# Attention over selected keys: exponentials turned unscaled, the softmax factor applied to a pair's output, one output bank

## The reference, cut to what matters

```python
def dsa_attention(h, w_in, q_gain, k_gain, w_uv, w_out, rel_bias):
    ...
    def block(args):
        ...
        _, sel = lax.top_k(isc, topk)
        valid = sel <= t[None, :, None]
        kg = k[bidx, sel]
        vg = vals[bidx, sel]
        logits = jnp.einsum('bqhd,bqkd->bqhk', qb, kg) * scale
        bias = rel_bias[t5_bucket(t[None, :, None] - sel)]
        logits = logits + jnp.swapaxes(bias, -1, -2).astype(jnp.float32)
        logits = jnp.where(valid[:, :, None, :], logits, NEG_2)
        p = jax.nn.softmax(logits, axis=-1)
        return jnp.einsum('bqhk,bqkd->bqhd', p, vg)

    ...
    o = jnp.einsum('bshl,hlv->bshv', o_lat, w_uv.astype(jnp.float32))
    return o.reshape(B, S, DSA_HEADS * DSA_V_DIM).astype(h.dtype) @ w_out
```

## Time and profile before

| | |
|---|---|
| median of three runs | 1922.81 us (1921.42 to 1926.16) |
| profiled execution, own time | 1924.47 us |
| its span, first to last instruction | 1922.7 us |
| PE busy | 1891.4 us, 98% of the span |
| DVE, ACT, POOL busy | 1071.2, 530.6, 1178.2 us |
| mean granted clock of TensorE | 0.995 of full speed |
| attention stage, first score to first product of the output projection | 1421.9 to 1512.5 us |

### The profile page before, as it was taken

One profiled execution on the slowest core, in us unless ns is written; L12 is line 12 of the kernel. 1 busy time (PEld: TensorE's weight loads), 2 busy tenths in 40 slices (PEclk: granted clock), 3 DMA queues, 4 the chain that ended last, 5 costly groups with the idle time before them and its releaser, 6 DMA issues.

```text
span 1922.7 us, 27358 instructions
## 1 busy us (share of the span) xinstructions
PE 1891.4 (98%) x9550; PEld 1539.9 (80%) x9550; DVE 1071.2 (56%) x1750; ACT 530.6 (28%) x1120; POOL 1178.2 (61%) x680
## 2 busy tenths in 40 slices
PE   9999999999999999999999999999989999999999
PEld 7867788888888877779888888876866798888887
DVE  5966589877785515555534342145988454343422
ACT  4135310000115424442211121033367331111110
POOL 7641688887665564335766666655764447666673
PEclk9999899999999999999999999999999999999999
DMA  7530277776552232124332333312210123332231
GB/s 278 196 103 12 68 272 252 249 240 218 197 175 68 86 110 62 48 62 158 110 98 91 95 98 99 98 64 80 86 58 2 34 66 120 98 98 92 94 98 66
DMA packets 62328, 221.06 MB, mean 115 GB/s; under 512 B 6907, under 2 KB 7163, under 8 KB 62124
## 3 DMA queue, kind: packets, MB, share of 16 engines
q1 hardware_dynamic: 45216, 161.58, 26.7%
q10 hardware_dynamic: 17036, 58.46, 8.4%
HBM read 217.87 MB, written 2.14 MB: 114 GB/s over the span
## 4 chain that ended last, share of the span: by engine, by line
PE 93%; DVE 3%; POOL 2%; issue 2%; ACT 1%; DMA 0%; SPq 0%; POOLq 0%; DVEq 0%; ACTq 0%
PE bank L321 25%; PE bank L323 25%; PE bank L322 25%; PE bank L921 2%; PE bank L580 1%; PE bank L356 1%; PE bank L361 1%; PE bank L1050 1%; PE bank L357 1%; PE bank L1102 1%; PE bank L1093 1%; PE bank L943 1%; PE bank L426 1%; PE bank L427 1%; PE bank L430 1%
## 5 line engine op out<-in xcount | busy, mean ns | idle before, releaser
L1558 POOL TENSOR_TENSOR w_lo<-raw,w_hi 128x1024 fp32r<-128x1024 f32 (+1 forms) x304 | 762.5, 2509 | 24.8
L321 PE MATMUL bank<-a_hi,w_hi 128*128 128x512 f32 (+1 forms) x2016 | 767.8, 381 | 0.8 <-POOL w_lo L1558 0.5
L322 PE MATMUL bank<-a_lo,w_hi 128*128 128x512 f32 (+1 forms) x2016 | 765.4, 380 | 0.0
L323 PE MATMUL bank<-a_hi,w_lo 128*128 128x512 f32 (+1 forms) x2016 | 765.4, 380 | 0.0
L1553 POOL TENSOR_SCALAR w_hi<-raw 128x1024 fp32r<-128x1024 f32 x298 | 341.4, 1146 | 608.7 <-PE bank L323 459.8
L321 PEld LDWEIGHTS bank<-a_hi,w_hi 128*128 128x128 f32 x2016 | 379.8, 188 | 72.5 <-POOL w_lo L1558 0.9
L323 PEld LDWEIGHTS bank<-a_hi,w_lo 128*128 128x128 f32 x2016 | 379.7, 188 | 71.3
L322 PEld LDWEIGHTS bank<-a_lo,w_hi 128*128 128x128 f32 x2016 | 379.9, 188 | 70.5
L2122 DVE SCALAR_TENSOR_TENSOR tmp<-bank,vecs,tmp 128x511 f32<-128x511 f32 x88 | 65.9, 749 | 240.9 <-ACT tmp L1828 240.8
L2107 DVE CUSTOM_DVE_ANT_0 y<-y,cond 128x1024 f32<-128x1024 f32 x84 | 197.7, 2388 | 0.0
L1828 ACT ACTIVATE tmp<-bank,vecs 128x512 f32<-128x512 f32 x88 | 68.1, 779 | 351.1 <-PE bank L323 347.2
(11 more groups left out here) (306 smaller groups left out, 2117.1 us busy)
## 6 DMA issues: line engine op xcount, KB each, us to landing
raw<-in_stream SPq DMA_DIRECT2D x299, 512.0 KB, 3.6
y<-in_ada ACTq DMA_DIRECT2D x96, 512.0 KB, 4.5
x<-in_x SPq DMA_DIRECT2D x4, 512.0 KB, 6.7
bias<-in_bias ACTq DMA_DIRECT2D x1, 2048.0 KB, 13.8
y<-rel_rows ACTq DMA_DIRECT2D x1, 2048.0 KB, 8.0
bias<-rel_rows ACTq DMA_DIRECT2D x1, 2048.0 KB, 14.4
out<-x SPq DMA_DIRECT2D x8, 256.0 KB, 2.0
cond<-in_c ACTq DMA_DIRECT2D x1, 512.0 KB, 6.5
```

The costliest lines, as they stand in the source:

```text
L321: pe.matmul(o, lhs_hi, rhs_hi, start=start, stop=False, **kw)
L322: pe.matmul(o, lhs_hi, rhs_lo, start=False, stop=False, **kw)
L323: return pe.matmul(o, lhs_lo, rhs_hi, start=False, stop=stop, **kw)
L1558: m = pool.tensor_tensor(w_lo[:, s, part], raw[:, j, part], f32(w_hi[:, s, part]), ALU.subtract)
```

## The change

The rows of scores are no longer scaled. ACT writes the exponentials straight into `tmp`, which frees the score bank; PE transposes them, and the outputs are sums of unscaled weights. For each pair DVE makes eight reciprocals in one instruction, widens them to a 128 by 512 tile (`factor_columns`), PE transposes that tile in four squares into bank 7, ACT copies it to `factor_rows`, and DVE multiplies the pair's output bank by it in place (`scaled`) before ACT and DVE round it as before. Bank 7 now holds the factor, so all pairs share output bank 6, and the wait for the low part of pair k stands ahead of pair k + 1. An output run now covers two blocks (four units) at a distance of six steps: two runs for a pair instead of four. Of the eight transposed units of a pair DVE copies three (units 1, 3 and 5) and ACT five; they have a place for every unit of a pair. The ring of tables has three buffers, since `first_rows` holds transposed units now. The new distances are in the diff. The new counters and the declaration of `factor_columns` are left out there, and so are the calls.

```diff
@@ -899,21 +900,43 @@
                         evacuate(u // 8 - 1)
...
         def score_bank(u):
...
-        D_NORM, D_TURN, D_COPY, D_OUT, D_HIGH, D_LOW = 2, 4, 3, 5, 9, 11
-        def pe_attention(pe, sems, units, queries, keys, values, probs, evacuated, ready=()):
+        def turned_bank(u):
+            return bank[(3, 5)[u % 2]]
+        factor_bank, d_out = bank[7], bank[6]
+        factor_rows = squares[:, 0, :]
+        def copied_by_dve(u):
+            return u % 8 in (1, 3, 5)
+        def d_probs(u):
+            i, side = u % 8 // 2, u % 2
+            return (probs_t[:, 2 + side, 384:512], first_rows[:, 256 * side:256 * side + 256], probs_t[:, 2 + side, 0:384], probs_t[:, side, :])[i]
+        def pair_ends(u):
+            return u >= 0 and u % 8 == 7
+        D_RECIPROCAL, D_TURN, D_COPY, D_COPY_DVE, D_SPREAD, D_FACTOR, D_OUT, D_SCALE, D_HIGH, D_LOW = 2, 4, 4, 4, 4, 4, 6, 7, 8, 9
+        def pe_attention(pe, sems, units, queries, keys, values, probs, base, evacuated, ready=()):
             n = len(units)
+            def copied(u):
+                mine = copied_by_dve(u)
+                pe.wait_ge(sems["copied_dve" if mine else "copied_act"], sum(copied_by_dve(k) == mine for k in range(u + 1)))
             for step in range(n + D_OUT):
...
-                        pe.wait_ge(sems["normed"], step - 3)
+                        pe.wait_ge(sems["exp"], step - 3)
                     if step == 3:
                         for counter, value in ready:
@@ -922,34 +945,44 @@
                 if D_TURN <= step < n + D_TURN:
                     u = step - D_TURN
                     h, i = units[u]
-                    pe.wait_ge(sems["normed"], u + 1)
+                    pe.wait_ge(sems["exp"], u + 1)
                     if u >= 2:
-                        pe.wait_ge(sems["copied"], u - 1)
+                        copied(u - 2)
                     for j in range(i + 1):
-                        m = pe.transpose(bank[(3, 5)[u % 2]][:, j * P:(j + 1) * P], tmp[:, u % 4, j * P:(j + 1) * P], ident)
+                        m = pe.transpose(turned_bank(u)[:, j * P:(j + 1) * P], tmp[:, u % 4, j * P:(j + 1) * P], ident)
                     m.then_inc(sems["turned"], 1)
+                u = step - D_SPREAD
+                if pair_ends(u):
+                    pe.wait_ge(sems["widened"], u // 8 + 1)
+                    if u > 7:
+                        pe.wait_ge(sems["factor"], u // 8)
+                    for i in range(TT):
+                        m = pe.transpose(factor_bank[:, i * P:(i + 1) * P], factor_columns[:, i * P:(i + 1) * P], ident)
+                    m.then_inc(sems["spread"], 1)
                 u = step - D_OUT
-                if u >= 0 and u % 2:
...
+                if u >= 0 and u % 4 == 3:
+                    h = units[u][0]
+                    copied(u - 1)
+                    copied(u)
+                    if h >= 2 and u % 8 == 3:
+                        pe.wait_ge(*evacuated(h // 2 - 1))
+                    for first in (u - 3, u - 1):
+                        i = units[first][1]
+                        for j in range(i + 1):
+                            for side in range(2):
+                                o = d_out[64 * side:64 * side + 64, i * P:(i + 1) * P]
+                                m = pe.matmul(o, values(h - 1 + side, j), probs(first + side)[:, j * P:(j + 1) * P], start=j == 0, stop=j == i)
+                                if j == i:
+                                    m.then_inc(sems["out"], 1)
+        def dve_attention(v, sems, units, tables, base, probs, low, prepared):
             n = len(units)
             for step in range(n + D_LOW):
-                u = step - D_LOW
-                if u >= 0 and units[u][0] % 2 and units[u][1] == TT - 1:
-                    low(v, units[u][0] // 2)
                 if step < n:
                     h, i = units[step]
                     cols = P * (i + 1)
@@ -962,40 +995,64 @@
                     b = score_bank(step)[:, 0:cols]
                     v.tensor_tensor_reduce(b, b, table, -1.0, 3e38, ALU.add, ALU.min,
                                            neg_max[:, base + step:base + step + 1]).then_inc(sems["masked"], 1)
-                u = step - D_NORM
...
+                u = step - D_COPY_DVE
+                if 0 <= u < n and copied_by_dve(u):
+                    cols = P * (units[u][1] + 1)
+                    v.wait_ge(sems["turned"], u + 1)
+                    if u >= 8:
+                        v.wait_ge(sems["out"], u - 7)
+                    v.tensor_copy(probs(u)[:, 0:cols], turned_bank(u)[:, 0:cols]).then_inc(sems["copied_dve"], 1)
+                u = step - D_RECIPROCAL
+                if pair_ends(u) and u < n:
                     v.wait_ge(sems["exp"], u + 1)
-                    v.reciprocal(rden[:, base + u:base + u + 1], den[:, base + u:base + u + 1]).then_inc(sems["rden"], 1)
...
+                    pair = slice(base + u - 7, base + u + 1)
+                    v.reciprocal(rden[:, pair], den[:, pair]).then_inc(sems["rden"], 1)
+                    v.wait_ge(sems["rden"], u // 8 + 1)
+                    if u > 7:
+                        v.wait_ge(sems["spread"], u // 8)
+                    v.tensor_scalar(factor_columns[:].rearrange("p (n s) -> p n s", n=8), rden[:, pair].unsqueeze(2).broadcast_to([P, 8, 64]),
+                                    1.0, None, ALU.mult).then_inc(sems["widened"], 1)
+                u = step - D_SCALE
+                if pair_ends(u) and u < n:
+                    v.wait_ge(sems["out"], u + 1)
+                    v.wait_ge(sems["factor"], u // 8 + 1)
+                    v.tensor_tensor(d_out[:], d_out[:], factor_rows, ALU.mult).then_inc(sems["scaled"], 1)
+                u = step - D_LOW
+                if pair_ends(u):
+                    low(v, u // 8)
...
         def act_attention(a, sems, units, probs, base, evacuate):
...
                     cols = P * (units[step][1] + 1)
-                    b = score_bank(step)[:, 0:cols]
                     a.wait_ge(sems["masked"], step + 1)
-                    a.activation(b, b, ACT.Exp, bias=neg_max[:, base + step:base + step + 1],
+                    if step >= 4:
+                        a.wait_ge(sems["turned"], step - 3)
+                    a.activation(tmp[:, step % 4, 0:cols], score_bank(step)[:, 0:cols], ACT.Exp, bias=neg_max[:, base + step:base + step + 1],
                                  scale=-1.0, accum_out=den[:, base + step:base + step + 1]).then_inc(sems["exp"], 1)
+                u = step - D_HIGH
+                if pair_ends(u):
+                    a.wait_ge(sems["scaled"], u // 8 + 1)
+                    evacuate(a, u // 8)
                 u = step - D_COPY
-                if 0 <= u < n:
+                if 0 <= u < n and not copied_by_dve(u):
                     cols = P * (units[u][1] + 1)
                     a.wait_ge(sems["turned"], u + 1)
-                    if u >= 4:
...
+                    if u >= 8:
+                        a.wait_ge(sems["out"], u - 7)
+                    a.activation(probs(u)[:, 0:cols], turned_bank(u)[:, 0:cols], ACT.Copy).then_inc(sems["copied_act"], 1)
+                u = step - D_FACTOR
+                if pair_ends(u) and u < n:
+                    a.wait_ge(sems["spread"], u // 8 + 1)
+                    if u > 7:
+                        a.wait_ge(sems["scaled"], u // 8)
+                    a.activation(factor_rows, factor_bank[:], ACT.Copy).then_inc(sems["factor"], 1)
@@ -1611,9 +1668,9 @@
             pool.wait_ge(selected, TT)
             for n, (h, i) in enumerate(masked_units):
                 cols = P * (i + 1)
-                if n >= 4:
-                    pool.wait_ge(d_sems["masked"], d_units.index(masked_units[n - 4]) + 1)
+                if n >= 3:
+                    pool.wait_ge(d_sems["masked"], d_units.index(masked_units[n - 3]) + 1)
                 pool.tensor_tensor(table_buf(n)[:, 0:cols], d_table(h, cols), not_selected[:, i, 0:cols], ALU.add).then_inc(table_ready, 1)
                 if n == 3:
                     split_stream(START["out3"] + 3, START["out3"] + 4)
@@ -2093,9 +2150,9 @@
                     a.activation(big[:, 16 + 2 * t + h, :], bank[t][:], ACT.Copy).then_inc(banks_free["act"], 1)
             def d_evacuate(a, c):
-                a.activation(a_hi[:, c, :], bank[6 + c % 2][:], ACT.Copy).then_inc(hi_ready, 1)
+                a.activation(a_hi[:, c, :], d_out[:], ACT.Copy).then_inc(hi_ready, 1)
             place_queries(3, range(2))
-            act_attention(a, d_sems, d_units, lambda u: probs_t[:, u % 4, :], n_stat // 2, d_evacuate)
+            act_attention(a, d_sems, d_units, d_probs, n_stat // 2, d_evacuate)
             act_halved_norm(a, "out3", "ffn1", lambda c: mod(1, 3, c))
             act_conv(a, 1)
             act_split_hidden(a, "down3")
```

(22 more changed lines are left out.)

18 lines of the change are left out of this document (2 added, 16 removed).

## The result

| | before | after |
|---|---|---|
| median of 7 runs each | 1922.81 us (1921.42 to 1926.16) | 1930.64 us (1929.79 to 1934.29) |
| ratio, 95% interval | | 1.004 (1.003 to 1.005) |
| span of the profiled execution | 1922.7 us | 1928.8 us |
| PE busy | 98% | 98% |

A forecast was written before the change was run, and what follows sets the result against it. PE, busy 98% of the span, was taken as the bound. Start +0.4, six pairs of +0.76 and end +0.85 gave +5.8 us on the 1922.81 median: 1928.6 us, range 1920 to 1933.

The forecast's parts named there:

- The chain of seven links: From unit 6's maximum through multiplication, exponential and high part to the low part; PE goes on at 5.27 us, period 11.61.
- w: PE's wait in each pair before its first output run, for the low part of the pair before: 1.81 us.
- no other wait of PE over 0.3: Sign of being right: besides seven waits of 1.8 us for the low part, PE waits nowhere over 0.3 us.
- a wait before transposes: Sign of being wrong: PE's waits stand before scores or transposes instead of ahead of the output products.
- +0.4: Start of stage: three table buffers delay tables and split by about 0.55 us; second pair's unit 6 comes 0.4 later.
- +0.85: End of stage: last run waits for ACT's copies; projection's first product 9.65 us after last unit 6, not 8.80.
- The sum: Whole stage: start 0.4, six pairs of 0.76 and end 0.85 make +5.8 us.
- Without any wait a pair costs 9.78: PE's own work in a pair of the changed kernel: 9.78 us, 1.07 less than 10.85.
- the first rival: PE never waits for the low part, w near 0: -6.9 us, 1915.9, faster; chance 0.13.
- Two runs fewer save 0.72: PE in each pair: an output run costs 0.36 us beside its products, so two fewer save 0.72.
- The third rival: More waiting on DVE: the widening waits for a POOL table, 3.5 us more, 1932.1; chance 0.20.
- The rule on rotating banks: Output banks: product groups should rotate through PSUM banks so evacuation overlaps the next products; by it the time is 1928.6 us.

The follow-up runs named there:

- e1: Changed kernel with ACT's high part ahead of unit 7's exponential and DVE's low part a step earlier: pair 10.74 us, ratio 1.0009 to the kernel before.
- e3: Changed kernel with POOL's split of one weight block moved from behind the fourth table to behind the ninth: stage 95.64 us, ratio 1.0023 to the kernel before.
- e2: Changed kernel with two output banks in turn and three score banks: pair 10.91 us, ratio 1.0017 to the kernel before.
- e7b: e5b with POOL's split of one weight block moved late: pair 10.41 us, stage 85.73, ratio 0.9975 to the kernel before.
- e8b: e2 with four output runs for a pair instead of two: pair 10.74 us, ratio 1.0007 to the kernel before.
- e4: Changed kernel without the factor (no reciprocals, widening, its transposes and copy, or multiplication): pair 11.29 us, ratio 1.0028 to the kernel before.
- e10: Changed kernel, one output bank, ACT's high part and copies before its exponential, low part a step earlier, split late: pair 10.56 us, ratio 0.9972 to the kernel before.
- e5b: e2 with ACT's copies moved ahead of its exponentials: pair 10.41 us, ratio 1.0000 to the kernel before.
- e9: e7b with DVE's copies moved ahead of its maxima: pair 10.66 us, ratio 0.9978 to the kernel before.

## Why the prediction was right, and where it was off

1. *The chain of seven links: right.* Each link was within 0.04 us. The run came at 5.33 (forecast 5.27), the rest of the pair took 6.38 (6.34), and the period was 11.71 (11.61). e1 shows that this chain is the cause: it moves one link, and 0.97 goes from each pair. By starts w was 1.87 (forecast 1.81). But 0.71 of it stands in another place, before unit 4's transposes, with 0.51 of idle time. The prediction had "no other wait of PE over 0.3" and named a wait before transposes as a sign of being wrong, and this sign came: ACT's copy of unit 2, behind the exponential of unit 6, was a second late thing that the chain covered. It did not change the sum, since the chain sets the end of both, and the period was within the 0.3 of 11.6.
2. *"+0.4" for the start: mis-sized, +2.08 measured.* I moved the split by 0.55 (0.69 measured from the first scores) and added that up. I had not asked how long PE would then stand, and what its clock would do: 3.47 us idle and 3.3 us at 0.51. e3 takes both away, and puts about 1.5 of the 2.08 down to the slow stretch; the rest is near the forecast.
3. *"+0.85" for the end: mis-sized, +2.05 measured.* The waiting was forecast, the work at 0.50 behind it not. e1, which removes the waits, has 8.77. In e3 the waits and the slow end both stay (11.20).
4. *The sum: +5.8 forecast, +9.3 in the stage, +7.8 by the medians.* The 3.5 between forecast and stage are the start (2.08 - 0.4 = 1.7), the end (2.05 - 0.85 = 1.2) and the six pairs (5.16 - 4.56 = 0.6). The stage's 9.3 lies inside the interval of the ratio (0.3% to 0.5%, 5.8 to 9.6 us), so medians and stage do not contradict each other. That the median came within 2.0 of the forecast is in part luck: the stage, which has less noise, was off by 3.5. The direction and the mechanism were right, and the size was short by the terms at both ends.
5. *"Without any wait a pair costs 9.78": the price was right, a pair without waits never came.* Taking off what PE lost by starts leaves 9.84 in the kernel after (11.71 - 1.87) and 9.81 in e2 and e7b. But no kernel came under 10.41. Since the first rival's price took all waits as gone, a kernel that never waits for the low part was worth +2.6 us by the medians (e2), not -6.9. The step that failed is that nothing else is late once the low part is not: ACT's copies were, by 1.10 of each pair (e2), and behind them DVE's copy of unit 3, by 0.60 (e7b).
6. *"Two runs fewer save 0.72": not realised.* That price holds where PE has no gaps. In e8b the two further runs cost nothing, because they fill one.
7. *The widening: 0.43 where I took 0.7.* POOL was idle beside it. The third rival did not occur. The multiplication took 0.73 (0.70), and by e4 costs the chain 0.16.
8. *The rule on rotating banks* (the Trainium skill, Perfetto Trace Analysis, Optimizing Tensor Performance, Matmuls): the time went its way, but e1 and e10 show that it was not the number of banks that decided: in the order of the kernel after a second bank takes 0.80 us off a pair, and moving the high part alone, with one bank, 0.97.

## What to carry to other kernels

Where queues are in order, follow the chain that gives a buffer back, and put each link ahead of the unrelated work of its engine; here that was worth more than the second buffer (0.97 against 0.80 us of a pair). An engine's order has to be tried link by link, though: moving ACT's copies ahead gained 0.50 (e5b), and moving DVE's too lost 0.25 of it (e9). A saving on the bounding engine is worth only what is left once the next late thing has been priced, so price that one as well. And an idle of the matmul engine must be counted with the work at the lower clock behind it.

## What the runs showed of the hardware

- An idle of 3.47 us cost about 1.5 us beyond itself, in 3.3 us of work at a granted clock of 0.51.
- At the end of the stage the clock fell to 0.50 although no single idle was over 1.23 us. The waits of 1.11 and 0.51 in the steady pairs did not do it (1.00 throughout).
- One and the same code can run at another mean clock in another execution. Between 580 and 600 us, which no edit touches, the granted clock was 1.00 in the profiled executions of after, e2, e4 and e10, whose stage begins at 1418.7 to 1419.0, and 0.84 to 0.91 in the eight others, whose stage begins at 1421.9 to 1422.8. Differences of spans of a few us say little here; differences between two points of a stage say more.
